# The last three output strips of a two-block kernel, computed in two halves of the tokens

## The chip, the cores and the metric

The kernel runs on one core of one Trainium2 chip. The metric is the time of one execution on the device in microseconds (us), from start to end. Lower is better. All data is float32; 512 tokens pass through two transformer-like blocks of width 1024.

## The reference

The whole reference is two blocks. The first has gated attention, a recurrence, a cross attention and a feed-forward part; the second has a convolution branch, a state-space branch and a gated feed-forward part. Only the end of the second block matters here:

```python
def rms_norm(x, g):
    xf = x.astype(jnp.float32)
    y = xf * lax.rsqrt(jnp.mean(xf * xf, axis=-1, keepdims=True) + RMS_EPS)
    return (y * g.astype(jnp.float32)).astype(x.dtype)

    # second block, last lines; x is (1, 512, 1024)
    x = x + rms_norm(mixed, mix_post_g[i])
    h = rms_norm(x, ffn_pre_g[i])
    gt, up = jnp.split(h @ w_gate_up[i], 2, axis=-1)     # two of 2816 columns
    f = (jax.nn.silu(gt) * up) @ w_down[i]               # 2816 -> 1024
    x = x + rms_norm(f, ffn_post_g[i])
return x
```

The mean inside `rms_norm` goes over the 1024 features of one token, so no token's last norm is known until all features of that token are. Two tokens don't depend on each other in these lines.

## The kernel before

Everything is held with the features on the 128 partitions: a "tile" is 128 features by all 512 tokens, and a matrix of width 1024 is 8 tiles (`KT = 8`, `S = 512`). A weight matrix comes as a stream of 314 strips. A strip is the weights of one output tile: 128 columns by up to 8 k-blocks of 128 rows. Each strip is loaded twice from device memory: by SyncE into `raw`, from which ScalarE writes the rounded high part `wh` and the negated copy `wl`, and by GpSimd as a transfer that adds the weights onto `wl` (the low part). TensorE then makes three products for each k-block (high x high, high x low, low x high, lines 390 to 392) into one of four PSUM banks, bank `j % 4` for strip `j`, and VectorE takes the bank out. TensorE waits for a bank through `bank_free`, VectorE for a strip through `strip_done`. Order is written out by hand: each engine has one program, and the programs meet only at semaphores.

The last feed-forward matrix (`down`) is summed in three chunks of the hidden width. The last chunk has six k-blocks, so each of its 8 strips is 6 x 3 = 18 matmuls of 512 columns. In this chunk, for output tile `n`, VectorE adds the bank onto `acc` (line 2430; `acc` lies in the tensor that the profile calls `arena`), ScalarE squares it (line 1010) and VectorE adds the squares into `ssum` (`sum_square`, line 1567). The square of the eighth tile is not added by VectorE; TensorE takes it straight from `sq`.

After the last strip comes a chain of small steps. `norm_cols` (line 454) sums the squares over the partitions with one-column matmuls, first from `ssum`, then from the last `sq`; ScalarE takes the square root (line 1024), VectorE the reciprocal (line 1587), `norm_spread` (line 463) spreads the four columns of factors over all partitions by matmuls. VectorE then scales all 8 tiles. For the first five (`BY_PE = 5`) it only scales `acc` in place (line 2441), and TensorE adds the old residual `h` and the scaled tile in PSUM by products with the identity (`old_residual`, line 890, and line 899); ScalarE copies the sum to `h` (line 1524). For the other three VectorE scales into `xt` (line 2445) and adds to `h` (line 2447). SyncE stores each finished tile, 256 KB, to the output (`store`, line 954), in the order 0, 1, 2, 5, 3, 6, 4, 7, and waits for all stores at the end. GpSimd has nothing to do after the last `wl` transfer (line 972).

Of the kernel before, what the change touches and what calls it, by code (L numbers as in the profile page):

```python
# [6 lines left out]
P = 128  # L7
S = 512
# [161 lines left out]
BY_PE = 5  # L170
SUBBED = sorted(DIRECT + LOCAL)
# [17 lines left out]
def block_kernel(nc, xT, memT, weights, weights6, vectors, consts, scratch, spill, outT):  # L189
    with ExitStack() as ctx:  # L190
# [148 lines left out]
        for name, tiles, sqs, norms in [  # L339
            ("in", KT, KT, 1), ("mem", KT, 0, 1), ("rec", 4, 0, 0), ("fox", 4, 0, 0), ("w_out", KT, KT, 1),  # L340
            ("xattn", KT, 0, 0), ("xo", KT, KT, 1), ("hid", 4 * KT, 0, 0), ("final", 0, KT, 1),
            ("pre", KT, 0, 1), ("y0", KT, 0, 0), ("y1", KT, 0, 0), ("conv", KT, KT, 2),
            ("mix", KT, 0, 0), ("post", 0, KT, 1), ("ffn", KT, KT, 1),
            ("g0", KT, 0, 0), ("g1", KT, 0, 0), ("g2", CHUNK2[2], 0, 0), ("ffpost", 0, KT, 1),
        ]:
            XN[name], SQN[name], NORM[name] = nx, nsq, nn
            nx, nsq, nn = nx + tiles, nsq + sqs, nn + norms
# [22 lines left out]
        def _(pe):  # L370
# [495 lines left out]
            for c, nt in enumerate(CHUNK2):  # L866
# [13 lines left out]
                for n in range(KT):  # L880
                    strip(AT[f"down{c}"] + n, XB, kts=range(nt), xn=tiles_from(f"g{c}", nt) if n == 0 else None)
            sums = [work[0], work[1], bank[0], bank[1], bank[2]]

            def old_residual(n):

                if n > 1:
                    pe.wait_ge(bank_free[n - 2], sum(j % 4 == n - 2 for j in range(NS)))
                elif used[n]:
                    pe.wait_ge(wk_free[n], used[n])
                mm(sums[n][:, :], ident, tile(h, n), start=True, stop=False)  # L890
# [12 lines left out]
        def _(sp):  # L903
# [49 lines left out]
            def store(n):  # L953
                sp.dma_start(outT[:, n * S:(n + 1) * S], tile(h, n)).then_inc(sem("stored"), 16)
# [7 lines left out]
            sp.wait_ge(sem("stored"), 16 * KT)  # L962


        @block.gpsimd
        def _(pool):
# [8 lines left out]
            for j in range(NS):  # L975
                if j not in SUBBED:
                    low(j)


        @block.scalar  # L980
        def _(act):
# [522 lines left out]
            for c, nt in enumerate(CHUNK2):  # L1504
# [9 lines left out]
                for n in range(KT):  # L1514
                    if c == 2 and n == KT - 1:
                        root_table()
                    step(AT[f"down{c}"] + n)
                    if c == 2:
                        square(tile(acc, n), n, SQN["ffpost"] + n)
            root_cols(NORM["ffpost"])  # L1520
            sums = [work[0], work[1], bank[0], bank[1], bank[2]]
            for n in range(BY_PE):
                act.wait_ge(sem("out_sum"), n + 1)
                act_(tile(h, n), sums[n][:, :], ACT.Copy)
# [4 lines left out]
        def _(dve):  # L1529
# [865 lines left out]
            for c, nt in enumerate(CHUNK2):  # L2395
# [28 lines left out]
                for n in range(KT):  # L2424
# [6 lines left out]
                    if c == 2:  # L2431
                        dve.drain().then_inc(h_upd, 1)
                        if n < KT - 1:
                            sum_square(n, SQN["ffpost"] + n)
                            if n == KT - 2:
                                dve.drain().then_inc(ssum_rdy, 1)
                dve.drain()
            cols_recip(NORM["ffpost"])
            r = wait_full(dve, ("spread", NORM["ffpost"]))
            for n in range(BY_PE):  # L2440
                STT(tile(acc, n), tile(acc, n), V("ffpost_g", n), r[:, :], ALU.mult, ALU.mult)
                dve.drain().then_inc(sem("out_x"), 1)
            for n in range(BY_PE, KT + 1):
                if n < KT:
                    STT(xt[:, n % 2, :], tile(acc, n), V("ffpost_g", n), r[:, :], ALU.mult, ALU.mult)
                if n > BY_PE:
                    TTop(tile(h, n - 1), tile(h, n - 1), xt[:, (n - 1) % 2, :], ALU.add)
# [72 lines left out]
```

## Time and profile before

| | us |
|---|---|
| median of 3 runs | 1924.39 |
| lowest and highest run | 1921.95, 1924.89 |
| the profiled execution's own time | 1923.32 |
| its span, first to last instruction | 1921.5 |
| TensorE busy | 1884.3 (98% of the span) |
| VectorE busy | 1025.0 (53%) |
| ScalarE busy | 1085.0 (56%) |
| GpSimd busy | 255.9 (13%) |
| mean granted TensorE clock | 0.995 |

The span is a single profiled execution; the profiled execution's own time is 1.8 us longer than its span. All starts below are microseconds from the start of the span. PE is TensorE, PEld its weight loads, DVE VectorE, ACT ScalarE, POOL GpSimd, SP SyncE. An engine name with a q is that engine's sequencer. The times of matmuls overlap, since they are pipelined, so their pitch (from one start to the next) tells more than their duration.

### The profile page before, as it was taken

To read this page: it belongs to the slowest core of one execution; us is meant where nothing else is said; L and a number is where in the kernel's file an instruction comes from. 1 tells how busy PE (TensorE), PEld (TensorE's weight loads), DVE (VectorE), ACT (ScalarE), POOL (GpSimd) and SP (SyncE) were. 2 spreads that over 40 slices of the span, in tenths; PEclk is the share of its full clock that TensorE was granted. 3 is DMA by queue.
4 is the path that set the end of the run, shared out by engine and by line. 5 is a ranking of instruction groups with operands and counts; after the bars stand their busy time and mean duration, and the time that the engine had idled before them with its cause. 6 is when DMAs were issued, how large, how long until landed. Compare 5 with 4: busy or idle time off the path is not lost.

```text
span 1921.5 us, 26190 instructions
## 1 busy us (share of the span) xinstructions
PE 1884.3 (98%) x9286; PEld 1551.6 (81%) x9286; DVE 1025.0 (53%) x1695; ACT 1085.0 (56%) x1512; POOL 255.9 (13%) x299
## 2 busy tenths in 40 slices
PE   7999999999999999999999999999999999999999
PEld 6877788887888888878878888888888878888886
DVE  5566663455413233358878888788633273133134
ACT  7655666535433333554589997798574544344343
POOL 0110011100111111111111111111111101111110
PEclk9999999999999999989999999999999989999999
DMA  7854468854989898869787778877889839989884
GB/s 231 192 133 109 121 177 201 180 111 114 192 192 193 196 191 193 192 133 212 177 188 185 174 170 212 205 170 173 220 184 200 187 94 211 191 196 191 195 177 114
DMA packets 94346, 339.99 MB, mean 177 GB/s; under 512 B 10488, under 2 KB 10488, under 8 KB 93984
## 3 DMA queue, kind: packets, MB, share of 16 engines
q0 software_dynamic: 42480, 153.64, 44.2%
q1 hardware_dynamic: 47232, 169.14, 30.8%
q10 hardware_dynamic: 4528, 15.81, 2.3%
q8 instruction: 65, 1.06, 0.2%
q14 instruction: 41, 0.34, 0.1%
HBM read 334.27 MB, written 4.28 MB: 176 GB/s over the span
## 4 chain that ended last, share of the span: by engine, by line
PE 80%; DVE 9%; ACT 4%; DMA 3%; issue 2%; ACTq 1%; DVEq 1%; SPq 0%
PE bank L390 20%; PE bank L392 20%; PE bank L391 20%; DVE ssum L2119 5%; PE bank L515 2%; PE bank L516 2%; PE bank L517 2%; DMA wl<-in_weights 1%; PE work L470 1%; PE bank L405 1%; PE bank L407 1%; PE bank L406 1%; DMA raw<-in_weights 1%; ACT wl L993 1%; PE work L685 1%
## 5 line engine op out<-in xcount | busy, mean ns | idle before, releaser
L992 ACT ACTIVATE wh<-raw 128x1024 fp32r<-128x1024 f32 x295 | 312.2, 1058 | 593.7 <-PE bank L392 511.4
L390 PE MATMUL bank<-XAh,wh 128*128 128x512 f32 x1384 | 546.4, 395 | 11.4 <-DVE XAl L1605 8.5
L392 PE MATMUL bank<-XAh,wl 128*128 128x512 f32 x1384 | 540.0, 390 | 0.0
L391 PE MATMUL bank<-XAl,wh 128*128 128x512 f32 x1384 | 539.9, 390 | 0.0
L972 POOL DMA_DIRECT2D wl<-in_weights x295 | 255.7, 867 | 1636.4 <-ACT wl L993 1600.1
L390 PEld LDWEIGHTS bank<-XAh,wh 128*128 128x128 f32 x1384 | 260.5, 188 | 68.8 <-DVE wl L1545 8.7
L993 ACT ACTIVATE wl<-raw 128x1024 fp32r<-128x1024 f32 x295 | 307.8, 1043 | 0.0
L392 PEld LDWEIGHTS bank<-XAh,wl 128*128 128x128 f32 x1384 | 260.5, 188 | 55.5
L391 PEld LDWEIGHTS bank<-XAl,wh 128*128 128x128 f32 x1384 | 260.7, 188 | 53.5 <-issue 0.7
L390 PE MATMUL bank<-XBh,wh 128*128 128x512 f32 x720 | 281.4, 391 | 0.4 <-DVE wl L1552 0.4
L392 PE MATMUL bank<-XBh,wl 128*128 128x512 f32 x720 | 280.2, 389 | 0.0
L391 PE MATMUL bank<-XBl,wh 128*128 128x512 f32 x720 | 280.1, 389 | 0.0
L2119 DVE SCALAR_TENSOR_TENSOR ssum<-arena,vec,ssum 128x512 f32<-128x512 f32 x232 | 174.4, 752 | 22.8 <-issue 6.0
L390 PEld LDWEIGHTS bank<-XBh,wh 128*128 128x128 f32 x720 | 135.1, 188 | 29.4 <-DVE wl L1552 0.8
L391 PEld LDWEIGHTS bank<-XBl,wh 128*128 128x128 f32 x720 | 135.2, 188 | 28.4 <-issue 0.5
L392 PEld LDWEIGHTS bank<-XBh,wl 128*128 128x128 f32 x720 | 135.1, 188 | 28.3
L515 PE MATMUL bank<-XAh,wh 128*128 128x512 f32 (+1 forms) x256 | 93.9, 367 | 3.3 <-DMA wl<-in_weights 1.8
L517 PE MATMUL bank<-XAh,wl 128*128 128x512 f32 (+1 forms) x256 | 86.4, 337 | 0.0
L516 PE MATMUL bank<-XAl,wh 128*128 128x512 f32 (+1 forms) x256 | 86.3, 337 | 0.0
L2153 DVE SCALAR_TENSOR_TENSOR xt<-arena,vec,xt 128x512 f32<-128x512 f32 x96 | 72.2, 752 | 11.4 <-ACTq L1339 3.6
L2055 DVE TENSOR_TENSOR h<-h,bank 128x512 f32<-128x512 f32 x24 | 16.5, 688 | 107.9 <-PE bank L392 107.9
L2043 DVE SCALAR_TENSOR_TENSOR xt<-bank,rstd 128x512 f32<-128x512 f32 x32 | 22.1, 692 | 85.8 <-PE bank L392 85.5
(371 smaller groups left out, 2122.2 us busy)
## 6 DMA issues: line engine op xcount, KB each, us to landing
raw<-in_weights SPq DMA_DIRECT2D x294, 512.0 KB, 5.9
wl<-in_weights POOLq DMA_DIRECT2D x287, 512.0 KB, 7.9
arena<-scratch ACTq DMA_DIRECT2D x20, 512.0 KB, 5.5
wraw<-in_weights SPq DMA_DIRECT2D x12, 512.0 KB, 7.0
raw<-in_weights SPq DMA_DIRECT2D x8, 384.0 KB, 4.4
wl<-in_weights POOLq DMA_DIRECT2D x8, 384.0 KB, 6.0
h<-in_xT SPq DMA_DIRECT2D x4, 512.0 KB, 6.7
spill<-cst ACTq DMA_DIRECT2D x8, 256.0 KB, 6.8
```

The source lines that it names most:

```text
L390: mm(bank[s][:, 0:w], hi, tile(X[0], k, w), start=(n == 0), stop=False)
L391: mm(bank[s][:, 0:w], hi, tile(X[1], k, w), start=False, stop=False)
L392: last = mm(bank[s][:, 0:w], lo, tile(X[0], k, w), start=False, stop=(n == len(kts) - 1))
L515: mm(bank[b][:, 0:w], hi, tile(XA[0], k, w), start=(k == 0), stop=False)
L516: mm(bank[b][:, 0:w], hi, tile(XA[1], k, w), start=False, stop=False)
L517: last = mm(bank[b][:, 0:w], lo, tile(XA[0], k, w), start=False, stop=(k == KT - 1))
L972: pool.dma_start(wl[j % 4][:, 0:w.shape[1]], w, accum_op=ALU.add).then_inc(w_lo[j % 4], 16)
L992: act_(wh[j % 4][:, :], raw[a % 2][:, :], ACT.Copy)
L993: act_(wl[j % 4][:, :], raw[a % 2][:, :], ACT.Copy, scale=-1.0).then_inc(raw_free[a % 2], 1)
L2043: leave(STT(xt[:, u % 2, :], ps[:, :], 0.0, rstd[:, :], ALU.max, ALU.mult), j)
L2119: STT(v[:, 0:S] if k == 0 else c, v[:, k:k + S], V("dw_w", t * CONV_K + k), c, ALU.mult, ALU.add)
L2153: STT(x, rawp[:, k % 2, tap:tap + S], V("sc_w", ct * SK + tap), x, ALU.mult, ALU.add)
```

## The change

The last three strips (`HALVED = 3`: tiles 5, 6, 7) of the last chunk are each multiplied in two halves of 256 tokens (`HALF = 256`): first the early half of tiles 5, 6, 7, then the late half of tiles 5, 6, 7. Both halves of a strip use the same bank (each its own 256 columns) and the same weights.

- TensorE: six half strips of 18 matmuls of 256 columns. Inside the late half of tile 5, after 4 of its 6 k-blocks, it sums the squares of the early half (`half_norm(0)`); inside the late half of tile 6, at the same place, it spreads the early factors (`half_spread(0)`). After the last half strip the same steps follow for the late half, and the residual sums of tiles 0 to 4 take 256 columns in place of 512.
- VectorE: takes each half out of its bank (`half_taken`), sums the squares of each half (`half_sum`), and scales the early halves of all 8 tiles in place (`scale_early`: tiles 0 and 1 before the late sum of tile 6, tiles 2 and 3 after it, tiles 4 to 7 after it has taken the late half of tile 7). After that come the late reciprocal and the late scaling and adding, as before with half the columns.
- ScalarE: squares and roots by halves; the square root's table is now loaded after the early square of tile 6.
- GpSimd: two transfers add the scaled early halves (`acc`) onto `h`, tiles 0 to 3 and tiles 4 to 7, 512 KB each in rows of 1 KB (`half_x`, `half_sum`). When both have landed, two more transfers store the early halves of `h`, 512 KB each, to the output.
- SyncE: stores only the late half of each tile, 128 KB, and waits at the end also for GpSimd's two stores.

The diff, shortened (what is left out is a repetition of what the list above says):

```diff
@@ TensorE @@
-                for n in range(KT):
+                for n in range(KT - (HALVED if c == 2 else 0)):
                     strip(AT[f"down{c}"] + n, XB, kts=range(nt), xn=tiles_from(f"g{c}", nt) if n == 0 else None)
+            def half_strip(j, part, amid=None):
+                b, t0 = j % 4, part * HALF
+                if part == 0:
+                    low_ready(j)
+                pe.wait_ge(bank_free[b], j // 4 + part)
+                out = bank[b][:, t0:t0 + HALF]
+                for k in range(CHUNK2[2]):
+                    hi, lo = wh[b][:, k * P:(k + 1) * P], wl[b][:, k * P:(k + 1) * P]
+                    mm(out, hi, tile(XB[0], k)[:, t0:t0 + HALF], start=(k == 0), stop=False)
+                    mm(out, hi, tile(XB[1], k)[:, t0:t0 + HALF], start=False, stop=False)
+                    last = mm(out, lo, tile(XB[0], k)[:, t0:t0 + HALF], start=False, stop=(k == CHUNK2[2] - 1))
+                    if k == 3 and amid:
+                        amid()
+                last.then_inc(strip_done if part else sem("half_done"), 1)
...
+            for part in range(2):
+                for n in range(KT - HALVED, KT):
+                    amid = {(1, KT - 3): lambda: half_norm(0), (1, KT - 2): lambda: half_spread(0)}.get((part, n))
+                    half_strip(AT["down2"] + n, part, amid)
...
-            norm_cols(NORM["ffpost"], SQN["ffpost"] + KT, between=lambda: old_residual(0))
+            half_norm(1, between=lambda: old_residual(0))
             old_residual(1)
-            norm_spread(NORM["ffpost"], 5)
+            half_spread(1)
             for n in range(BY_PE):
                 if n > 1:
                     old_residual(n)
                 pe.wait_ge(sem("out_x"), n + 1)
-                mm(sums[n][:, :], ident, tile(acc, n), start=False, stop=True).then_inc(sem("out_sum"), 1)
+                mm(sums[n][:, 0:HALF], ident, tile(acc, n)[:, HALF:], start=False, stop=True).then_inc(sem("out_sum"), 1)
@@ SyncE @@
-                sp.dma_start(outT[:, n * S:(n + 1) * S], tile(h, n)).then_inc(sem("stored"), 16)
+                sp.dma_start(outT[:, n * S + HALF:(n + 1) * S], tile(h, n)[:, HALF:]).then_inc(sem("stored"), 16)
...
             sp.wait_ge(sem("stored"), 16 * KT)
+            sp.wait_ge(sem("half_stored"), 32)
@@ GpSimd @@
+            def halves(a, q):
+                return a[:, :].rearrange("p (n s) -> p n s", s=S)[:, 4 * q:4 * q + 4, 0:HALF]
+            for q in range(2):
+                pool.wait_ge(sem("half_x"), 4 * q + 4)
+                pool.dma_start(halves(h, q), halves(acc, q), accum_op=ALU.add).then_inc(sem("half_sum"), 16)
+            for q in range(2):
+                pool.wait_ge(sem("half_sum"), 32)
+                pool.dma_start(halves(outT, q), halves(h, q)).then_inc(sem("half_stored"), 16)
@@ ScalarE @@
+            for n in range(KT - HALVED, KT):
+                half_square(n, 0)
+                if n == KT - 2:
+                    root_table()
+            half_root(0)
+            for n in range(KT - HALVED, KT):
+                half_square(n, 1)
+            half_root(1)
@@ VectorE @@
+            def half_taken(n, part):
+                j = AT["down2"] + n
+                if part:
+                    leave(TTop(late(n), late(n), taken(j)[:, HALF:], ALU.add), j)
+                else:
+                    dve.wait_ge(sem("half_done"), n - (KT - HALVED) + 1)
+                    leave(TTop(early(n), early(n), bank[j % 4][:, 0:HALF], ALU.add), j)
+                dve.drain().then_inc(h_upd, 1)
...
+            def scale_early(tiles):
+                r = wait_full(dve, ("spread", NORM["ffpost"]))
+                for n in tiles:
+                    ins = STT(early(n), early(n), V("ffpost_g", n), r[:, 0:HALF], ALU.mult, ALU.mult)
+                    if n == KT - 1:
+                        free(ins, ("spread", NORM["ffpost"]))
+                    if n % 4 == 3:
+                        dve.drain().then_inc(sem("half_x"), 4)
+            a, b, c = range(KT - HALVED, KT)
+            half_taken(a, 0)
+            half_sum(a, 0)
+            half_taken(b, 0)
+            half_sum(b, 0)
+            dve.drain().then_inc(ssum_rdy, 1)
+            half_taken(c, 0)
+            half_recip(0)
+            half_taken(a, 1)
+            half_sum(a, 1)
+            half_taken(b, 1)
+            scale_early(range(2))
+            half_sum(b, 1)
+            dve.drain().then_inc(ssum_rdy, 1)
+            scale_early(range(2, 4))
+            half_taken(c, 1)
+            scale_early(range(4, KT))
+            half_recip(1)
+            r = wait_full(dve, ("spread", NORM["ffpost"] + 1))
             for n in range(BY_PE):
-                STT(tile(acc, n), tile(acc, n), V("ffpost_g", n), r[:, :], ALU.mult, ALU.mult)
+                STT(late(n), late(n), V("ffpost_g", n), r[:, 0:HALF], ALU.mult, ALU.mult)
                 dve.drain().then_inc(sem("out_x"), 1)
```

## Rows read from the trace of the kernel before

**Rows 1.** The page: shares of the chain that ended last, by engine.

```profile
PE 80%; DVE 9%; ACT 4%; DMA 3%; issue 2%; ACTq 1%; DVEq 1%; SPq 0%
```

**Rows 2.** Busy time in four stretches of the end; instruction counts in brackets, transfer share last.

```profile
1893.10:1905.34 12.24, 12.24 (x57) 10.13 (x56) 4.15 (x6) 3.38 (x5) 0.00 (x0) 1.00 0.21 32
1905.34:1909.78 4.44, 4.40 (x28) 3.12 (x27) 0.87 (x3) 0.89 (x2) 0.00 (x0) 1.00 0.02 4
1909.78:1918.57 8.79, 7.14 (x16) 2.88 (x16) 7.87 (x11) 2.98 (x5) 0.00 (x0) 1.00 0.39 150
1918.57:1921.50 2.93, 0.00 (x0) 0.00 (x0) 0.00 (x0) 0.00 (x0) 0.00 (x0) 1.00 0.70 268
```

**Rows 3.** The chain that ended last, in time: start, us, what.

```profile
1905.34 0.79 PE work L454 x8
...
1906.12 0.97 PE work L890 x2
...
1908.85 0.91 PE work L463 x8
...
1909.78 0.75 DVE arena L2441
...
1910.64 0.75 DVE arena L2441
...
1916.40 0.75 DVE xt L2445
...
1917.88 0.69 DVE h L2447
```

**Rows 4.** The timeline of the end: start, us, engine, line, operation, idle before.

```profile
1902.71 1.28 ACT L1028 ACT_TABLE_LOAD   x1
...
1905.38 0.69 DVE L2430 TENSOR_TENSOR arena<-arena,bank 128x512 f32<-128x512 f32 x1 [1.96 <-PE bank L392]
...
1906.14 0.63 ACT L1010 ACTIVATE sq<-arena 128x512 f32<-128x512 f32 x1 [1.93 <-DVEq L2432]
...
1907.92 0.26 ACT L1024 ACTIVATE small<-work,cst 128x4 f32<-128x4 f32 x1 [1.14 <-PE work L454]
1908.21 0.18 DVE L1587 RECIPROCAL small<-small 128x4 f32<-128x4 f32 x1 [2.15 <-ACT small L1024]
```

**Rows 5.** The timeline of TensorE at 297 us, where strips have 256 columns.

```profile
297.13 0.28 PE L515 MATMUL bank<-XAh,wh 128*128 128x256 f32 x1
297.25 0.28 PE L516 MATMUL bank<-XAl,wh 128*128 128x256 f32 x1
```

**Rows 6.** Groups by shape, whole span: busy us, mean ns of one, idle before.

```profile
L1936 DVE TENSOR_TENSOR xt<-bank,arena 128x256 f32<-128x256 f32 x8 | 3.4, 422 | 7.1 <-PE work L470 5.0 <-PE bank L517 1.7 <-issue 0.4
...
L1791 DVE SCALAR_TENSOR_TENSOR XAl<-arena,vec,XAh 128x256 fp32r<-128x256 f32 x4 | 1.8, 481 | 0.1
...
L1068 ACT ACTIVATE early<-early 128x256 f32<-128x256 f32 x28 | 11.5, 411 | 0.0
```

**Rows 7.** The last adding transfer: timeline, first bytes (40 slices of 1892.9 to 1893.4), landing.

```profile
1890.42 1.04 ACT L993 ACTIVATE wl<-raw 128x1024 fp32r<-128x1024 f32 x1
...
1891.76 0.86 POOL L972 DMA_DIRECT2D wl<-in_weights  x1 [3.62 <-ACT wl L993]
...
DMA  0000000000000000000000000000000000099000
...
wl<-in_weights POOLq DMA_DIRECT2D x1, 384.0 KB, 4.7
...
L972 POOL DMA_DIRECT2D wl<-in_weights x295: 862/862/1305, 27.8 to 1891.8; - x148
```

**Rows 8.** Queue, packets, MB, share of 16 engines: 1894.5 to 1895.5, 1138.5 to 1139.8, 1918.9 to 1920.4.

```profile
q0 software_dynamic: 70, 0.22, 111.5%
...
q0 software_dynamic: 66, 0.27, 104.1%
...
q1 hardware_dynamic: 328, 0.61, 104.8%
```

**Rows 9.** Transfers busy in 40 slices of 1918.5 to 1922.

```profile
DMA  1489999999999999999999981000000000000000
```

More of the change, by code:

```diff
@@ new lines, in half_norm @@
+            def half_norm(part, between=None):
+                w, t0 = work_bank(("norm", NORM["ffpost"] + part), 3), part * HALF
+                done = SQN["ffpost"] + KT + part * HALVED
+                pe.wait_ge(ssum_rdy, NORM["ffpost"] + part + 1)
+                for n, summed in enumerate((ssum, sq[:, 1, :])):
+                    if n:
+                        if between:
+                            between()
+                        pe.wait_ge(sq_done, done)
+                    for c in range(TT // 2):
+                        last = mm(w[:, c:c + 1], summed[:, t0 + c * P:t0 + (c + 1) * P], ones[:, 0:1],
+                                  start=(n + c == 0), stop=(n == 1 and c == TT // 2 - 1))
+                last.then_inc(wk_done[3], 1)
@@ new lines, in half_spread @@
+            def half_spread(part):
+                w = work_bank(("spread", NORM["ffpost"] + part), 2)
+                pe.wait_ge(sem("n_rr"), 5 + part)
+                for c in range(TT // 2):
+                    at = part * TT // 2 + c
+                    last = mm(w[:, c * P:(c + 1) * P], s_nr[:, at:at + 1].broadcast_to([P, P]), ident, start=True, stop=True)
+                last.then_inc(wk_done[2], 1)
+            for part in range(2):
+                for n in range(KT - HALVED, KT):
+                    amid = {(1, KT - 3): lambda: half_norm(0), (1, KT - 2): lambda: half_spread(0)}.get((part, n))
+                    half_strip(AT["down2"] + n, part, amid)
@@ L886, in old_residual @@
                 if n > 1:
-                    pe.wait_ge(bank_free[n - 2], sum(j % 4 == n - 2 for j in range(NS)))
+                    pe.wait_ge(bank_free[n - 2], sum(j % 4 == n - 2 for j in [*range(NS), *range(NS - HALVED, NS)]))
                 elif used[n]:
                     pe.wait_ge(wk_free[n], used[n])
-                mm(sums[n][:, :], ident, tile(h, n), start=True, stop=False)
-            norm_cols(NORM["ffpost"], SQN["ffpost"] + KT, between=lambda: old_residual(0))
+                mm(sums[n][:, 0:HALF], ident, tile(h, n)[:, HALF:], start=True, stop=False)
+            half_norm(1, between=lambda: old_residual(0))
             old_residual(1)
-            norm_spread(NORM["ffpost"], 5)
+            half_spread(1)
             for n in range(BY_PE):
@@ L1523, in _ @@
                 act.wait_ge(sem("out_sum"), n + 1)
-                act_(tile(h, n), sums[n][:, :], ACT.Copy)
+                act_(tile(h, n)[:, HALF:], sums[n][:, 0:HALF], ACT.Copy)
                 act.drain().then_inc(sem("result_pe"), 1)
@@ L2423, in _ @@
                 k += nt
-                for n in range(KT):
+                for n in range(KT - (HALVED if c == 2 else 0)):
                     j = AT[f"down{c}"] + n
@@ new lines, in late, with half_sum @@
+            def late(n):
+                return tile(acc, n)[:, HALF:]
+            def half_taken(n, part):
[6 more added lines that the diff above has]
+                dve.drain().then_inc(h_upd, 1)
+            def half_sum(n, part):
+                cols = slice(part * HALF, (part + 1) * HALF)
+                dve.wait_ge(sq_done, SQN["ffpost"] + n + part * HALVED + 1)
+                TTop(ssum[:, cols], ssum[:, cols], sq[:, n % 2, cols], ALU.add)
+                dve.drain()
@@ new lines, in half_recip @@
+            def half_recip(part):
+                wait_read(dve, ("norm", NORM["ffpost"] + part))
+                nc.vector.reciprocal(s_nr[:, 2 * part:2 * part + 2], s_nr[:, 2 * part:2 * part + 2])
+                dve.drain().then_inc(sem("n_rr"), 1)
+            def scale_early(tiles):
[6 more added lines that the diff above has]
+                        dve.drain().then_inc(sem("half_x"), 4)
```

29 lines of the change are left out of this document (16 added, 13 removed).

## The prediction

> **What bounds the kernel now.** I began with the page's chain: 80% of it is TensorE [rows 1], and the page has TensorE busy for 98% of the span, so strips follow one another without gaps and nothing that another engine does beside them costs time. What is left to win is at the end, so I cut the last 28 us into four stretches [rows 2]. The reader is to see that TensorE has no gap in the first (12.24 us busy of 12.24, three strips of 18 matmuls: 0.227 us a matmul), and that after the last strip, at 1905.34, 16.16 us follow before the span ends: 4.44 us for the norm, 8.79 us of scaling and adding, and 2.93 us from VectorE's last sum to the last landed store. The chain in time [rows 3] says who sets each: the norm is a sequence of small matmuls with VectorE, ScalarE and VectorE between them [rows 4]; the 8.79 us are VectorE's alone, at 0.87 us for each of five scalings and about 1.5 us for a scale and an add (1916.40 to 1917.88). The granted clock is 1.00 (its level of 2.4 GHz) in all four stretches.
>
> **TensorE, part by part.** Three strips of 54 matmuls become 108 matmuls of 256 columns. Where this kernel has such matmuls, with a new weight load each, one starts 0.12 us after another [rows 5]: 108 x 0.12 = 12.96 us against 12.24, +0.72. The weight loads, one for each matmul, set no higher floor there. Put inside the strips: `half_norm(0)`, 4 matmuls, which in the profile are 8 records at 0.79 us together, and `half_spread(0)`, half of 8 records at 0.91, so 0.46 [rows 3]. With 0.1 for two changes between kinds of matmul (taken; 0 to 0.5) the last half strip ends at 1893.10 + 12.96 + 0.79 + 0.46 + 0.1 = 1907.4, 2.1 us later than now. No wait is added to that: the last weights have landed at 1891.76 + 4.7 = 1896.5 [rows 7], and the early half of tile 7 starts at 1893.10 + 2 x 2.16 = 1897.4; the banks' early halves are out by then; the square needed by `half_norm(0)` at 1901.0 is there at 1900.5 (end of the early half of tile 7 at 1899.6, take 0.42, square 0.41). The table load of 1.28 us [rows 4] now stands after the early square of tile 6, near 1898.4, and is done before 1899.9, hidden under the half strips.
>
> **VectorE, up to the late factors.** A 256-column take or sum is 0.42 us, a scaling 0.48, a square on ScalarE 0.41 [rows 6]. The early factors' reciprocal ends near 1902.4, then late take of 5 (to 1903.0), its sum (1903.9), the late take of 6, for which TensorE is ready at 1905.2 (1905.7), scale 0 and 1 (1906.7), sum (1907.2), scale 2 and 3 (1908.2). `half_x` reaches 4 at 1908.3. Only now comes the late take of 7, 0.9 us after TensorE finished it: the scalings are in its way. It ends at 1908.7; ScalarE squares to 1909.2; TensorE's two sums and the root are done by 1910.0 (0.4 and 0.26 [rows 4], with gaps). But VectorE first scales tiles 4 to 7: four times 0.48 from 1908.75, to 1910.7, and `half_x` reaches 8 at 1910.75. The late reciprocal (0.18) waits behind them, so it ends at 1910.95. From there to the first scaling it is now 1909.78 - 1908.39 = 1.39 us with four spreading matmuls; with two it is 0.45 less, so 1911.9.
>
> **VectorE, the late half.** A scaling's pitch is now 0.867, of which 0.75 is the instruction [rows 3]; with 0.48 it is 0.60. Five are 3.0. The first of the other three is 0.56, then twice a scale and an add (1.48 now, 0.94 after), then an add, 0.42: in all 3.0 + 0.56 + 1.88 + 0.42 = 5.9, against 8.79. TensorE's residual sums (0.43 a product of 256 columns, by halving 0.86 of a pair of records) stay ahead of it. So VectorE's last sum ends at 1917.8, against 1918.57. The last store is 128 KB instead of 256, 0.3 us less than the 2.93 us [rows 2]: this chain alone would end the span at 1920.4, a gain of 1.1 us. All the halving bought here (4.2 us in this chain and in the norm's small steps, with the shorter store) is mostly paid back by TensorE's 2.1 us and the 1.6 us that the early scalings stand in the way.
>
> **GpSimd's chain, which is new.** Two adding transfers, then two stores that wait for both. Nothing of this kind is in the trace; the nearest is the last `wl` transfer, which had the transfer engines to itself. ScalarE ended at 1891.46, GpSimd's instruction began 0.3 us later, first bytes moved at 1893.35, 1.6 us after that, and it landed 4.7 us after the start [rows 7]. Packets: 70 of 3 KB took 111.5% of 16 us, 0.255 us each; 66 of 4 KB took 104.1% of 20.8 us, 0.328 each [rows 8]. The line through both is 0.073 us a KB and 0.036 fixed, so an adding packet of 1 KB is 0.109 us. Ends: 0.043 (an ordinary 2 KB packet of the stores is 0.085 with the small ones left out: 1.048 x 24 us / 296, halved [rows 8]) and 0.255 (no cheaper than the one of 3 KB). I take the line, since two sizes lie on it. A 512 KB transfer is 512 rows of 1 KB, 32 for each of 16 engines.
>
> First bytes of the first: 1908.3 + 0.3 + 1.6 = 1910.2; of the second 1910.75 + 1.9 = 1912.65, when the first is still under way. 64 x 0.109 = 7.0: 1917.2. By then SyncE has put some three late stores among them, 3 x 8 packets x 0.043 = 1.0: 1918.2. Landing 0.5 more (today's last bytes move at 1920.7, 0.8 before the span's end [rows 9]; 0.5 is my estimate of the receipt's part): 1918.7. The first store's instruction starts at 1919.0, its bytes at 1920.6; the second follows on the queue. 64 x 0.043 = 2.75: 1923.35, and 0.8 to the end: 1924.15. SyncE waits for it, and nothing covers it: the span would be 2.65 us longer. Bounds: with 0.043 for the adding packets the stores start 4.2 us earlier and VectorE's chain is last again (-1.1 us, or -0.8 with the two kinds of stores in each other's way); with 0.255 they start 64 x 0.146 = 9.3 us later (+12).
>
> GpSimd's instruction itself: 0.86 us with 128 rows, at 3 KB as at 4 KB, 1.3 at most [rows 7]. With 512 rows it may stay 0.86 or take four times as much, 3.45. I take 0.86, since bytes don't change it, and keep the other end for the range.
>
> The Trainium skill ("DMA: Bandwidth & Descriptors", section on the anatomy of a DMA of the gpsimd path) gives about 2.0 us + bytes / 436 GB/s for such a transfer: 2.9 us for the 384 KB that took 4.7 here, so the trace disagrees for adding ones. By that rule the adding transfers land near 1915 and the stores near 1920, and the time would be that of VectorE's chain, the rival A below. The same section says that many descriptors can be emitted before their cost shows; no run here shows it, and it speaks for 0.86.
>
> **The sum.** Profiled execution: 1923.32 + 2.65 = 1926.0. Its own time lies 1.07 below the median of the runs (within their 1921.95 to 1924.89), so on the median: 1924.39 + 2.7 = 1927.1. What a measurement can tell from no change is about 0.2%, 3.85 us: 1920.5 to 1928.2 is "same".
>
> **The rivals.** A, *adding within the core runs at a copy's speed*: the engines take 0.04 to 0.06 us for 1 KB, GpSimd's chain ends before 1920.4, and VectorE sets the end. For it: the adding rows measured read their source from device memory, these don't. Against it: the two rows give a slope of 0.073 us a KB, twice a copy's, which a nearer source need not change. 1924.39 - 1.1 = 1923.3. B, *slower than before: the 1 KB rows*. Either the four software transfers cost GpSimd 3.45 us each, one after another: the second is written out by 1915.5, the stores by 1919.0 + 6.9 = 1925.9, last bytes at about 1926.6, end 1927.4, +5.9, 1930.3; or each packet costs far more than the line says, and at 0.18 us it is + 64 x 0.071 = 4.5 more, 7.2, 1931.6. It counts as slower once GpSimd's last store lands after 1925.3, which is 1.2 us beyond my sum: an instruction of 1.5 us, or a packet of 0.13, decides. I put its time at 1931. For it: 512 rows in place of 128 is the one thing here no row shows. C, *the halving shows fully*: the transfers are quick and the late steps need less than halved rows say (fixed parts of the small steps gone, no scalings in the way): it needs 2.8 us beyond A, for which no row speaks.
>
> **Chances.** Forecast 0.42, A 0.17, B 0.36, C 0.05. With the runs' own scatter (3 us between lowest and highest), the forecast and A are mostly "same", with a part of the forecast over the edge and a part of A below it: faster 0.07, same 0.53, slower 0.40. The range goes from 1922.2 (A, less a run's scatter) to 1932.5 (most of B; the end at +12 is left out).
>
> **What would show it.** Matmuls of 256 columns at a pitch of 0.12, the last half strip's end near 1907.4 and VectorE's last sum near 1917.8, shifted by any drift before 1893. Two GpSimd instructions near 1908.6 and 1911, two near 1919 to 1920; packets on the software queue of about 0.11 us in 1911 to 1917. The span's last wait is SyncE's for GpSimd's stores, about 3.5 us after its own are in. Wrong would be: GpSimd's stores landing before SyncE's (A), GpSimd instructions well over 1 us (B), or a pitch near 0.18, which would push the last half strip back by another 6.5 us.

## The result, and the profile after

The changed kernel takes 1925.58 us (median of 14 runs, 1919.52 to 1930.29), the kernel before 1922.34 (14 runs, 1917.98 to 1928.37). The ratio is 1.0018, 95% interval 1.001 to 1.0027: slower, by 2 to 5 us. The forecast was +2.7 us, that is 1.0014. The prediction called everything within 0.2% of the kernel before "same"; 1.0018 lies just inside that, though its interval lies above 1. In absolute time the forecast of 1927.1 is 1.5 us high, because the kernel before took 1924.39 in the 3 runs it started from and 1922.34 in these 14.

Its profiled execution has a span of 1923.9 us (own time 1925.65). The two spans can't be compared at their ends, since executions differ by a microsecond or two before the change begins: VectorE starts to take tile 4's strip at 1893.14 in the profile before and at 1891.28 in this one. I count from there, and call the time from that take to the end of the span the **stretch** (the strip itself ends 0.04 us earlier, from which some expectations count). It was 28.3 us (1921.48 - 1893.14) and is 32.6 (1923.86 - 1891.28), 4.2 more. Each stretch in this document comes from one profiled execution; two profiles of one kernel (10 and 12 below) gave 27.1 and 27.2.

The stages of the end, answering to [rows 2] (engine busy times, then granted clock, share of the transfer engines, GB/s):

```profile
1891.24:1905.39 14.15, 14.15 (x120) 14.09 (x120) 6.19 (x15) 4.47 (x9) 0.00 (x0) 1.00 0.18 29
1905.39:1910.26 4.87, 3.46 (x18) 2.39 (x16) 3.07 (x9) 0.68 (x2) 2.61 (x2) 0.87 0.45 70
1910.26:1916.51 6.25, 5.69 (x15) 4.62 (x16) 4.94 (x11) 1.51 (x4) 1.50 (x2) 0.56 0.94 182
1916.51:1923.90 7.39, 0.47 (x3) 0.07 (x1) 0.00 (x1) 0.42 (x2) 0.05 (x1) 0.68 0.60 227
```

The strips take 14.15 us instead of 12.24, the norm 4.9 instead of 4.4, VectorE's scaling 6.3 instead of 8.8, and then 7.4 us pass after VectorE's last add, where 2.9 did. That last stage is where the time went. Note the clock: 1.00 in all four stages before, 0.56 in the third now.

The timeline of the same end (start, us, engine, line; answers to [rows 3, 4]):

```profile
1905.39 0.58 PE L911 MATMUL work<-cst,ssum 128*128 128x1 f32 x4
...
1906.33 0.42 DVE L2519 TENSOR_TENSOR arena<-arena,bank 128x256 f32<-128x256 f32 x1
...
1908.68 0.17 DVE L2535 RECIPROCAL small<-small 128x2 f32<-128x2 f32 x1
...
1909.02 1.20 PE L921 MATMUL work<-cst,small 128*128 128x128 f32 x4 [0.57 <-DVEq L2536]
1910.26 2.88 DVE L2568 SCALAR_TENSOR_TENSOR arena<-arena,vec,work 128x256 f32<-128x256 f32 x5 [1.41 <-PE work L921]
...
1915.55 0.96 DVE L2574 TENSOR_TENSOR h<-h,xt 128x256 f32<-128x256 f32 x2
...
1917.02 0.38 ACT L1597 ACTIVATE h<-bank 128x256 f32<-128x256 f32 x1 [0.48 <-PE bank L945]
```

GpSimd's timeline, its adding packets in 1908 to 1910, and landings (answers to [rows 7, 8]):

```profile
1906.54 1.30 POOL L1031 DMA_DIRECT2D h<-arena  x1 [15.97 <-DVEq L2546]
1908.89 1.31 POOL L1031 DMA_DIRECT2D h<-arena  x1 [1.05 <-DVEq L2546]
1915.01 1.55 POOL L1034 DMA_DIRECT2D out<-h  x2 [4.82 <-DMA h<-arena]
...
q0 software_dynamic: 286, 0.29, 93.7%
...
out<-h SPq DMA_DIRECT2D x8, 128.0 KB, 3.2
out<-h POOLq DMA_DIRECT2D x2, 512.0 KB, 4.0
```

And the end of the program: the closing instructions of the engines (duration in ns, start), and what SyncE waited for.

```profile
L191 PEldq DRAIN  x1: 3815/3815/3815, 1913.2 to 1913.2; - x1
L191 POOLq DRAIN  x1: 8163/8163/8163, 1915.5 to 1915.5; - x1
...
L191 SPq DRAIN  x1: 7/7/7, 1921.6 to 1921.6; - x1
L191 SPq EVENT_SEMAPHORE  x1: 17/17/17, 1923.8 to 1923.8; - x1
...
SPq L191 <- PEq L191: 2.2, 1, 2.2
```

This is the line to read. SyncE had every store by 1921.6, GpSimd's too. Then it stood 2.2 us in the closing barrier. The profile names TensorE's sequencer as the last to arrive, but TensorE's drain was over at 1917.0; the one that ends when the barrier opens is GpSimd's drain, 1915.5 + 8.16 = 1923.7. In the kernel before, GpSimd's drain ran for 7.84 us too, but from 1891.7, and nobody saw it. The second store that GpSimd issued landed 4.6 us after 1915.8, at 1920.4; the drain ended 3.3 us after that. SyncE's own last store (instruction at 1918.2, landed 3.2 us later) came in at 1921.4, after both of GpSimd's. The last packets on the engines are SyncE's (window 1920.4 to 1921.2, nothing on the software queue):

```profile
q1 hardware_dynamic: 206, 0.18, 65.1%
```

Last, how busy the transfer engines are from 1908.4 to 1921.0, in tenths of 40 slices, changed kernel first, then before:

```profile
DMA  8999999996999999999970009699998999999996
```

```profile
DMA  0002000000000005959920039701999949999970
```

Where there were gaps between eight stores, there is now one load of adding packets up to 1914.3 (1 MB at 190 GB/s) and behind it nearly all of the 2 MB of output, late halves and early ones together.

### The profile page after: what moved, and what is told of

Same layout as the page of the kernel before. It is cut to its first block, busy times and chain, and to the rows that moved or that the text cites. A ratio compares the mean times of both kernels' runs of the same rounds, so it can differ in the third digit from the quotient of the medians.

```text
span 1923.9 us, 26332 instructions
## 1 busy us (share of the span) xinstructions
PE 1882.2 (98%) x9340; PEld 1554.9 (81%) x9340; DVE 1026.2 (53%) x1709; ACT 1085.1 (56%) x1516; POOL 259.4 (13%) x303
## 4 chain that ended last, share of the span: by engine, by line
PE 81%; DVE 9%; ACT 4%; DMA 2%; issue 2%; ACTq 1%; DVEq 1%; SPq 0%
PE bank L391 21%; PE bank L393 20%; PE bank L392 20%; DVE ssum L2192 5%; PE bank L516 2%; PE bank L518 2%; PE bank L517 2%; DMA wl<-in_weights 1%; PE work L471 1%; PE bank L406 1%; PE bank L408 1%; PE bank L407 1%; ACT wl L1050 1%; PE work L686 1%; DVE xt L2226 1%
## 5 line engine op out<-in xcount | busy, mean ns | idle before, releaser
L391 PE MATMUL bank<-XBh,wh 128*128 128x512 f32 x702 | 274.2, 391 | 0.4 <-DVE wl L1625 0.4
L393 PE MATMUL bank<-XBh,wl 128*128 128x512 f32 x702 | 273.1, 389 | 0.0
L392 PE MATMUL bank<-XBl,wh 128*128 128x512 f32 x702 | 273.1, 389 | 0.0
L392 PEld LDWEIGHTS bank<-XBl,wh 128*128 128x128 f32 x702 | 131.8, 188 | 27.7 <-issue 0.5
```

The lines of the kernel that those rows point to most:

```text
L391: mm(bank[s][:, 0:w], hi, tile(X[0], k, w), start=(n == 0), stop=False)
L392: mm(bank[s][:, 0:w], hi, tile(X[1], k, w), start=False, stop=False)
L393: last = mm(bank[s][:, 0:w], lo, tile(X[0], k, w), start=False, stop=(n == len(kts) - 1))
```

## The experiments

**Theory D** came first: GpSimd's closing drain ends the program. Its rival **P**: TensorE at 1.2 GHz and contending stores do. TensorE's clock has two levels here, 2.4 GHz (shown as 1.00) and 1.2 GHz (0.50).

*1. The early stores issued by SyncE.*

```diff
...
-            for q in range(2):                       # GpSimd
-                pool.wait_ge(sem("half_sum"), 32)
-                pool.dma_start(halves(outT, q), halves(h, q)).then_inc(sem("half_stored"), 16)
...
+                if n == 5:                           # SyncE, in the order of its late stores
+                    sp.wait_ge(sem("half_sum"), 32)
+                    for q in range(2):
+                        sp.dma_start(sp_halves(outT, q), sp_halves(h, q)).then_inc(sem("half_stored"), 16)
```

> The changed kernel, but the two stores of the early halves (512 KB each) are issued by SyncE, after its store of tile 5, and no longer by GpSimd. Theory D: the changed kernel ends with GpSimd's closing drain, which ends 7.1 us after GpSimd's last transfer instruction (1916.6 to 1923.7), while SyncE was done at 1921.6. Here that instruction is the second adding transfer (end at 1910.2 in the changed kernel's profile), so the drain is over near 1917.3 and the end is SyncE's: the span from the start of tile 5's early half (1891.5 there) to the end falls from 32.4 us to about 30.2, 2 us less, and the time is about that of the kernel before, ratio 0.9995 to 1.001. Theory P: the end was set by the late halves, with TensorE at its lower clock and stores that contend; then the stretch stays at 32.0 to 32.6 and the ratio stays at 1.0018.

```profile
L191 POOLq DRAIN  x1: 9052/9052/9052, 1909.0 to 1909.0; - x1
...
L191 SPq DRAIN  x1: 7/7/7, 1922.1 to 1922.1; - x1
```

The drain was over at 1918.05, 3.2 us after the second adding transfer landed, and SyncE set the end. Stretch 30.9, 1.7 less than the changed kernel; ratio 1.0013 (1.0003 to 1.0023). D holds for 1.7 of 4.2 us, but 2.6 are still there, so it was not the whole. The ratio alone decides nothing: it is above D's 1.001, and its interval holds P's 1.0018 too. The profile decides.

*2. One small late transfer in the kernel before.*

```diff
+            pool.wait_ge(sem("result"), 1)
+            pool.dma_start(scratch[0:16, 0:P], ident[0:16, 0:P]).then_inc(sem("late"), 16)
```

> The kernel before plus one 8 KB transfer from GpSimd to a scratch tensor, issued once VectorE's sum of tile 5 is out (1916.3 in the profile of before; the kernel otherwise has nothing of the change). Theory D, as a fixed 7 us after the instruction: GpSimd's instruction runs 1916.6 to 1917.4, its drain ends at 1924.5, and the span is 3.0 us longer, ratio about 1.0015. Theory D, as 3.2 us after the transfer has landed: it lands near 1918.6, the drain ends at 1921.8, 0.3 us longer, ratio 1.000 to 1.0003. Theory P: no drain that counts, no change.

```profile
scratch<-cst POOLq DMA_DIRECT2D x1, 8.0 KB, 2.2
...
L190 POOLq DRAIN  x1: 5355/5355/5355, 1913.0 to 1913.0; - x1
...
L190 SPq DRAIN  x1: 7/7/7, 1918.1 to 1918.1; - x1
```

Issued at 1913.05, landed at 1915.25, drain over at 1918.4: 3.15 us after the landing and 4.8 after the instruction's end, where the changed kernel had 7.1. So the drain follows the landing, by 3.1 to 3.3 us in all four profiles (before 3.1, changed 3.3, experiment 1 3.2, this 3.15). The ratio is 0.9999 (0.999 to 1.0009), which both the second form of D and P allow; the profile rules out the first form (a drain until 1920.7 here, 7.1 us after the instruction's end). The stretch was 29.0, 0.7 over before, of which the drain explains 0.3; the other 0.4 stay open.

*3. The early transfers left out.* GpSimd's two loops and SyncE's wait for `half_stored` are removed, so this kernel leaves out half of the output.

> The changed kernel without GpSimd's four transfers: the early halves are scaled, but neither added to h nor stored, so half of the output is left out. Theory D: GpSimd's drain is over long before, and SyncE's stores have the transfer engines to themselves: last copy of ScalarE 25.9 us after the start of tile 5's early half, its store issued 0.3 later and landed 2.0 after that, end near 28.5 us after that start against 32.4 with the transfers: 3.9 us less, ratio 0.9998. Theory P (TensorE's lower clock, 2 us of it in the late chain): the end falls only by what contention cost the stores, about 1.2 us, so 31.2 us and ratio 1.001.

```profile
out<-h SPq DMA_DIRECT2D x8, 128.0 KB, 1.7
...
L191 SPq DRAIN  x1: 7/7/7, 1919.0 to 1919.0; - x1
...
1908.92:1915.17 6.25, 5.68 (x13) 4.54 (x14) 4.93 (x11) 1.31 (x4) 0.00 (x0) 0.50 0.20 69
```

Stretch 28.8, ratio 1.0000 (0.9991 to 1.001). This kernel had the slow clock too (0.50 over VectorE's late scaling, as the last row above shows), so P's clock is not what cost 4.2 us: whatever it costs is already in this stretch, which is 3.8 us shorter than the changed kernel's (D said 3.9) and 0.5 longer than before. SyncE's stores land in 1.7 us where 3.2 was needed beside GpSimd's. The 4.2 us are thus: 0.5 for halves and their order, 2.1 for the four transfers in the way of the late stores (28.8 to 30.9), 1.7 for the two stores being GpSimd's (30.9 to 32.6). The 2.1 are P's other half, the contending transfers. The line between the last two shares is not sharp: in experiment 1 the early stores also start 1.1 us later after the take than in the changed kernel (24.8 against 23.7) and hold up SyncE's store of tile 3 behind them.

*4. The halves of the strips alone, in the kernel before.*

```diff
+                        for t0 in (0, S // 2):
+                            out = bank[b][:, t0:t0 + S // 2]
+                            for k in range(nt):
...
+                                mm(out, hi, tile(XB[0], k)[:, t0:t0 + S // 2], start=(k == 0), stop=False)
```

> The kernel before with one part of the change: strips 5 to 7 are multiplied in two halves of 256 columns each, one half right after the other, and everything else is as before. By the matmuls of 256 columns with a pitch of 0.12 us the three strips take 12.96 us instead of 12.24, 0.7 us more, ratio 1.0004. If the weight loads (0.19 us each in the records) were a floor, they would take 20.5 us, 8.3 more, ratio 1.0043.

```profile
1894.65:1907.60 12.95, 12.95 (x111) 12.95 (x110) 4.14 (x6) 3.38 (x5) 0.00 (x0) 1.00 0.18 32
```

12.95 us for 108 matmuls, 0.12 each, 0.7 more than before; the forecast had 12.96. The runs can't resolve it: 1.0000 (0.9991 to 1.001).

Then the question was whether the halves can win at all. **Theory T**: the adding transfers must go, since they keep the stores back and fill the engines. Its rivals are **S** (GpSimd's own adds hold VectorE up) and **L** (the late chain set the end anyway).

*5. GpSimd adds by instruction.*

```diff
...
-            for q in range(2):
-                pool.wait_ge(sem("half_x"), 4 * q + 4)
-                pool.dma_start(halves(h, q), halves(acc, q), accum_op=ALU.add).then_inc(sem("half_sum"), 16)
+            for p in range(4):
+                pool.wait_ge(sem("half_x"), 2 * p + 2)
+                nc.gpsimd.tensor_tensor(pairs(h, p), pairs(h, p), pairs(acc, p), ALU.add)
+                pool.drain().then_inc(sem("half_sum"), 1)
...
```

Left out above: GpSimd's two stores are removed, SyncE gets four in their place, and VectorE signals `half_x` after every second tile.

> The changed kernel with the same halves, but GpSimd adds the early halves to h with four instructions of its own (two tiles of 256 columns each), and SyncE stores them as four transfers of 256 KB before its late stores; no software transfer is left after the weights. Counted from the end of tile 4's strip to the end of the span (before 28.4 us, changed 32.7, without the early transfers 28.9). Theory T: what the changed kernel lost is that 1 MB of adding and then 2 MB of stores keep the 16 transfer engines busy without a gap from 1908.4 to 1921.0, and GpSimd's closing drain on top. Here 1 MB of stores is out before the late ones begin, so the stretch is 28.8 to 29.5 us and the ratio 0.9995 to 1.0008. Rival S: GpSimd's adds and VectorE's scalings share their way to memory, each scaling of 0.41 us takes 0.6 or more, late chain 1.5 us later: 30.5 us, ratio 1.001 or more.

VectorE's late sum of tile 6 in the changed kernel, then the same instruction here:

```profile
1904.74 0.42 DVE L2529 TENSOR_TENSOR ssum<-ssum,sq 128x256 f32<-128x256 f32 x1
```

```profile
1904.96 1.54 DVE L2533 TENSOR_TENSOR ssum<-ssum,sq 128x256 f32<-128x256 f32 x1
...
1904.95 1.26 POOL L1037 TENSOR_TENSOR h<-h,arena 128x512 f32<-128x512 f32 x1 [14.38 <-DVEq L2550]
1909.89 1.26 POOL L1037 TENSOR_TENSOR h<-h,arena 128x512 f32<-128x512 f32 x1 [3.67 <-DVEq L2550]
...
L1038 POOLq DRAIN  x4: 1332/1338/4848, 1904.9 to 1912.7; - x4
```

Stretch 29.9, ratio 1.0009 (1.0000 to 1.0018): half-way. S is right in one place and not where I put it: the scalings (one operand in SBUF, one in PSUM) kept their time (the five late ones, beside the adds, 2.88 us as in the changed kernel), but a sum of two SBUF operands beside GpSimd's add took 1.54 instead of 0.42. The Trainium skill ("SBUF — State Buffer", section on who interferes with whom) says that a VectorE instruction with two SBUF inputs contends with a GpSimd instruction that reads SBUF; the trace agrees. Second, GpSimd did nothing for 3.7 us between its first add and its second, though VectorE had tiles 2 and 3 ready at about 1907.6, 2.3 us before the second began; after the others it stood 0.2. The row of its drains says why: each starts with the add before it, three take 1.33 us, which is little more than the add's 1.26, and the first takes 4.85, 3.5 more. It is the first drain after the software transfers, though the last of those had landed at 1894.7, 10 us before it began.

*6. The same with VectorE's order changed* (late take of tile 7 before the early scalings of 2 to 4, late reciprocal before those of 5 to 7):

```diff
-            scale_early(range(2, 4))
             half_taken(c, 1)
-            scale_early(range(4, KT))
+            scale_early(range(2, 5))
             half_recip(1)
+            scale_early(range(5, KT))
```

> As the kernel with GpSimd's adding instructions, and VectorE takes the late half of tile 7 before it scales the early tiles 2 to 4, then makes the late reciprocal, and scales tiles 5 to 7 while TensorE spreads the factors. In the changed kernel the take came 1.0 us after TensorE was done, and the reciprocal 0.5 us after ScalarE's root. Theory T: with the transfer engines free the late chain sets the end, and 1.3 us of waiting leave it: 27.5 to 28 us of stretch, ratio 0.999 to 1.000. Rival S: as there, the scalings slow each other and the gain is under 0.5 us.

Stretch 29.6, ratio 1.0014 (1.0005 to 1.0023): theory T misses. The gain of 0.3 us is of the size that S gave, but the scalings did not slow (three with a drain of VectorE's between them take 1.47 us, as in experiment 7 without the adds). The reason shows in the next run.

*7. The changed kernel with this order only.*

> The changed kernel with GpSimd's four transfers as they are, and only VectorE's order changed: the late take of tile 7 before the early scalings of tiles 2 to 4, the late reciprocal before those of 5 to 7. Theory T: the transfer engines and the drain set the end, not the late chain; VectorE's last add comes 1.3 us earlier and the stretch stays within 0.4 us of 32.7, ratio 1.0015 to 1.002. Theory L (the late chain sets the end): the stretch is 1.3 us shorter, 31.4, ratio 1.001.

```profile
1910.00 1.22 PE L921 MATMUL work<-cst,small 128*128 128x128 f32 x4 [1.43 <-DVE arena L2542]
...
1908.21 1.30 POOL L1031 DMA_DIRECT2D h<-arena  x1 [16.94 <-DVEq L2546]
```

The reciprocal was done at 1908.6, but the spread began at 1910.0: it writes PSUM bank `work2`, which holds the early factors until VectorE's last early scaling. So the late chain did not move (first late scaling 19.1 us after tile 4's take, 19.0 in the changed kernel), and T and L could not be told apart by it as meant. Another thing moved instead: tiles 2 and 3 are scaled later, so the first adding transfer was issued 16.0 us after the take and no longer 15.3. The stretch grew from 32.6 to 33.2, ratio 1.0028 (1.0018 to 1.0039). With the late chain in place, 0.8 us later at the transfers was 0.7 later at the end: GpSimd's chain set the end. T's own bounds (within 0.4 us, ratio up to 1.002) were still missed a little, since it did not reckon with the later transfers.

*8. Filler matmuls while TensorE waits*, on kernel 6: 4 before the last squares' sum, 8 before the spread.

```diff
+            def filler(count):
+                for _ in range(count):
+                    mm(bank[3][:, 0:HALF], wh[3][:, 0:P], tile(XB[0], 0)[:, 0:HALF], start=True, stop=True)
```

> As the reordered kernel with GpSimd's adds, plus 12 matmuls of 256 columns whose result nobody reads, 4 while TensorE waits for the last square and 8 while it waits for the late reciprocal. In the changed kernel the granted clock fell to 0.5 (1.2 GHz) at 1909.0 after 3.6 us in which TensorE had gaps, the spread took 1.20 us for 4 records and a residual product 0.85 us a pair instead of 0.43. Theory C: with the gaps filled the clock stays at 1.00, the spread takes 0.5 and the pairs 0.43, ScalarE's last copy comes 0.8 to 1.5 us earlier and the stretch is 0.5 to 1 us under that without the fillers. Rival: the clock falls all the same, as TensorE waits between residual products anyway, and the fillers only delay the norm by 0.1 to 0.3 us.

```profile
1911.08 0.71 PE L921 MATMUL work<-cst,small 128*128 128x128 f32 x4 [1.08 <-DVE arena L2556]
...
1916.33 0.38 ACT L1611 ACTIVATE h<-bank 128x256 f32<-128x256 f32 x1 [0.48 <-PE bank L955]
```

The clock stayed at 1.00 to 1919.1 in this profile. The spread took 0.71 instead of 1.22, and ScalarE's last copy began 1.1 us earlier against the take than in kernel 6. C is right on the clock as far as one profile says, and worth nothing here: stretch 29.65, ratio 1.0018 (1.0008 to 1.0027), since VectorE was last. The six profiles of halved kernels without fillers so far (changed, 1, 3, 5, 6, 7) all show the fall, between 1908.6 and 1910.0. But kernels 10 and 11 below, also without fillers, kept 1.00 through their matmuls, so that it was the fillers that held the clock is not shown.

**Theory W**: three waits hold the halves back, all seen above.

*9 and 10. The waits removed, with and without the fillers.* The three together, so what each is worth by itself is not shown.

```diff
-                w = work_bank(("spread", NORM["ffpost"] + part), 2)
+                w = work_bank(("spread", NORM["ffpost"] + part), 2 + part)
...
+            pool.drain()                             # right after the last weights transfer
...
+            dve.drain().then_inc(sem("half_x"), 2)   # tiles 0 and 1: after the late sum of tile 6
```

> The kernel with GpSimd's adds, the new order and the 12 filler matmuls, with three obstacles taken away that its profile showed: the late factors go to PSUM bank work3 instead of work2 (TensorE waited 1.1 us for VectorE's last early scaling to free work2); GpSimd drains once right after its last weights transfer, so that its first add is not followed by 3.7 us without work; its first add starts after VectorE's late sum of tile 6 and no longer beside it (that sum came 1.2 us late in the three kernels with adds). Theory W (these three waits are what the order could not win): the first late scaling comes 17.6 us after the end of tile 4's strip (19.0 in the changed kernel, 20.7 in the kernel with fillers), the span ends 26.3 to 27 us after it (before 28.4, changed 32.7), ratio 0.9985 to 0.9995. Rival S: GpSimd's adds, now beside VectorE's take and scalings, hold these up too; then the stretch is 28 us or more and the ratio 1.000 or more.

> The same with the three obstacles taken away, without the filler matmuls. If the clock falls to 0.5 again after the gaps, the spread takes 0.4 us more and the residual products lag (0.85 us a pair), so ScalarE's last copy comes 1 us or more later and the stretch is 0.5 to 1 us longer than with fillers. If, with the waits gone, TensorE's gaps are short enough for the clock to stay at 1.00, it is equal or 0.2 us shorter, since the fillers are themselves in the way.

Kernel 10 by stages, as above:

```profile
1890.34:1904.50 14.16, 14.16 (x122) 14.11 (x120) 6.13 (x14) 4.47 (x9) 0.00 (x0) 1.00 0.16 28
1904.50:1908.48 3.98, 2.94 (x17) 1.97 (x16) 3.20 (x8) 0.68 (x2) 3.38 (x3) 1.00 0.19 68
1908.48:1914.74 6.26, 3.89 (x16) 2.88 (x16) 4.93 (x11) 1.92 (x5) 1.68 (x2) 1.00 0.61 213
1914.74:1917.50 2.76, 0.00 (x0) 0.00 (x0) 0.00 (x0) 0.00 (x0) 0.00 (x0) 0.56 0.52 181
```

Norm 4.0 us, tail 2.8: the halves now give more than they cost. The stretch is 27.7 with fillers and 27.1 without, against 28.3 before; ratios 0.9992 (0.9983 to 1.0002) and 0.9991 (0.9981 to 1.0002). Kernel 9 falls between its two forecasts: the first late scaling came 18.7 us after the take (W 17.6), the stretch is 27.7 (W 26.3 to 27, S 28 or more). What S feared did not happen, since VectorE's late take beside an add kept its 0.42 us. In kernel 10 the clock stayed at 1.00 through the matmuls without fillers too. That is the second case forecast for it, but it gave 0.6 us and not 0.2 at most: the fillers themselves had delayed the reciprocal, by 0.6 us.

*11 and 12. A sixth tile's residual on TensorE (`BY_PE = 6`), and kernel 10 again.*

> The unblocked kernel without fillers, with the late residual of a sixth tile (tile 5) summed by TensorE instead of VectorE (BY_PE = 6, its sum in the fourth PSUM bank), and SyncE's late stores in the order 0, 1, 2, 3, 4, 6, 7, 5. In that kernel VectorE's last add ended at 1914.7, TensorE's last residual product at 1912.9 and a tile costs TensorE 0.86 us, so both end near 1914: the stretch from the end of tile 4's strip falls from 27.1 us to 26.4 if VectorE was last there, and stays at 27.1 if the stores' packets (2 MB in rows of 1 KB) set the end. Ratio 0.9985 to 0.9995.

> The unblocked kernel without fillers once more, unchanged, on the chip of this call: its stretch was 27.1 us against 28.4 before, so the ratio should again be 0.999 (1.3 us of 1921 is 0.9993), and both calls together should tell whether it beats the kernel before.

The third stage of 11, then of 12:

```profile
1910.80:1916.70 5.90, 4.75 (x20) 3.63 (x20) 4.56 (x10) 2.31 (x6) 1.71 (x2) 1.00 0.65 228
```

```profile
1909.80:1916.00 6.20, 5.19 (x16) 4.03 (x16) 4.87 (x11) 1.92 (x5) 1.70 (x2) 0.72 0.60 210
```

Stretches 26.7 (between its two cases, 26.4 and 27.1) and 27.2 (forecast 27.1); ratios 0.9995 (0.9986 to 1.0004) and 0.9995 (0.9985 to 1.0005). In 12 the clock fell, and its stretch is still only 0.2 us longer than that of 10, not the 0.5 to 1 us that experiment 10 had put on the clock. The profiles put kernel 11 at 1.6 us and kernel 10 at 1.1 to 1.3 us under the kernel before, kernel 10 twice; the timed runs lean the same way four times but every interval reaches 1. The two ratios of the same kernel, 10 and 12, taken together give about 0.9993 (0.9986 to 1.0000, my estimate from the two intervals). Both beat the changed kernel, whose interval starts at 1.001. That they beat the kernel before is likely, not shown by the times.

## Why the prediction came out right, and where a step of it was wrong

Its times, moved by the 1.86 us between the two takes, against the profile after:

- *TensorE.* Last half strip's end 1905.5, measured 1905.4. The pitch of 0.12, the 0.7 us and the hidden table load and weights were right (experiment 4).
- *Scalings in the way.* The late take's end 1906.8 (1906.75 measured), the second `half_x` 1908.9 (GpSimd's instruction began then, so the signal came some 0.3 earlier; a scaling was 0.42 in a row, not 0.48). But taking them out of the way is not worth the 1.6 us that I put on them: a second wait, for PSUM bank `work2`, stood behind (experiments 6 and 7). I had read what each engine does next and not which bank the spread writes. A slip without effect on the sum: what the halving buys in that paragraph is 4.8 us by its own terms (2.9 in VectorE's chain, 1.6 in the norm, 0.3 for the store), not 4.2; only so do the 2.1 and 1.6 paid back leave its gain of 1.1.
- *The clock.* I took 1.00 from [rows 2] for the new tail. It fell to 0.5 (1.2 GHz) at 1909.0, after 3.6 us in which TensorE had gaps, until 1915.8. The spread took 1.20 us, a residual pair 0.85 instead of 0.43, and TensorE, which I had ahead of VectorE, fell behind, so that ScalarE's last copy ended 0.9 us after VectorE (1917.4, VectorE's last add at 1916.5, forecast 1915.9). This was hidden behind GpSimd's chain.
- *The adding packets.* First bytes 1908.3, measured 1908.4. 0.109 us by the line through 3 KB and 4 KB; 286 packets took 93.7% of 32 us, 0.105 each. The line held at a third of its shorter packet. The last moved at 1914.3 and not 1916.3. One of these 2 us is the three late stores that I had put among them: of SyncE's packets 42 had moved in 1912 to 1914.3. The other is that packets overlap on an engine (117% of the engines' time in that window), which the shares over 100% in [rows 8] had already shown and the sum left out. Rival A (a copy's speed) is out.
- *GpSimd's instruction.* 1.30 us for 512 rows, against 0.86 taken and 3.45 as the other end; B's point of 1.5 was not reached. Each store's was 0.78, with 512 rows too.
- *The stores* were on the engines until 1921.0, late halves among them, forecast 1921.5. GpSimd's own landed at 1920.4. They moved in packets of 4 KB (288 packets for 1.05 MB, 32 of them small), not in the 64 packets of 1 KB an engine that I had counted; with 49.4% of 5.2 us they took 2.6 us an engine against 2.75, so this term came out near for another reason.
- *The end.* Forecast 1922.3, measured 1923.9. The step that failed is "SyncE waits for it, and nothing covers it": GpSimd's stores landed 1.0 us before SyncE's last (1920.4 against 1921.4), where I had them 3.5 us after, and SyncE was through at 1921.6. By my own list this is a sign of being wrong, the one given for rival A; but A's cause was not there, and A's time neither. The closing drain, 3.3 us after the last software transfer landed, was no term of the sum and makes 2.1 us at the end of this profile. Transfers done 0.5 us sooner than forecast (1921.0 against 1921.5) hid part of that: the stretch grew by 4.2 us, the forecast was 2.7 (2.65 + 2.1 - 0.5 is the 4.2), and 2.7 is inside the measured 2 to 5.

The Trainium skill's formula ("DMA: Bandwidth & Descriptors", section on the anatomy of a DMA of the gpsimd path), 2.0 us and bytes / 436 GB/s, makes 3.2 us for 512 KB (an estimate). It was not met: 5.2 and 5.8 us for the adding ones, 3.5 and 4.6 for the stores, though only the first of the four had the engines to itself from its start.

So the direction came out for the reason given: GpSimd's chain sets the end (shown by 3 and 7), though by its drain and by standing in the way of the late stores, not by SyncE's wait for it. That the size came out is in part luck: the drain was missing from the sum (2.1 us), the transfers were put too late (the adding ones by 2.0, the last byte by 0.5), and the two have opposite signs.

## What to carry to other kernels

At the end of a program, a transfer issued by GpSimd cost its landing and 3.1 to 3.3 us more before the last barrier could open (changed kernel, experiments 1 and 2); issue the last stores from another queue, and look at each engine's closing drain in the profile, not at whom the barrier's wait is put down to. Before halving a stage to overlap it, count the transfer engines' work in the new tail: what is gained on VectorE is gone if a megabyte of adding stands ahead of the output. When work is reordered, list the buffers as well as the instructions; one PSUM bank kept the whole reorder from showing.

## What was not expected of the hardware

- GpSimd's drain ends 3.1 to 3.3 us after the landing of its last software transfer (four profiles). Even 10 us after such a landing the first drain took 4.85 us with the add before it and kept GpSimd idle for 3.7, 2.3 of them with its next work ready (experiment 5); a later one took 1.33 and kept it idle for 0.2.
- GpSimd's instruction for a transfer grew from 0.86 us (128 rows) to 1.30 (512 rows), not by four; a store of 512 rows took 0.78, so the rows alone do not set it.
- A VectorE sum of two SBUF operands beside a GpSimd add: 1.54 us instead of 0.42; scalings with one of them in PSUM: unchanged.
- The granted clock in the tail differs between executions of one kernel: kernel 10 kept 1.00 until 1915.1, past its last matmul at 1912.9, the same kernel in 12 fell at 1910.0 for 3.4 us. What decides there stays open.
